# Latent attention scores: three fp32r products of high and low parts in place of one fp32 product

## The chip, the core and the metric

The kernel runs on one core of one Trainium2 chip. The metric is device time in microseconds (us) of one execution; lower is better. TensorE is called PE here, VectorE DVE, ScalarE ACT, GpSimd POOL and SyncE SP.

## The reference, cut to what matters

The whole program is two transformer mixers on 512 tokens of width 2048, all in fp32: a sliding-window attention, and then a block with two attentions side by side, a differential one and a latent one (MLA), whose outputs are gated and projected. The change touches the scores of the latent one alone: eight heads, a 128-wide part without rotation (`nope`) and a 64-wide part with rotation (`pe`), 512 tokens and 16 meta keys in front of them.

```
def _mla_attention(q_nope, q_pe, k_nope, k_pe, v):
    L = k_nope.shape[2]
    scale = (B_NOPE + B_ROPE) ** -0.5
    k_pos = jnp.arange(L, dtype=jnp.int32)

    def block(start):
        qn = lax.dynamic_slice_in_dim(q_nope, start, Q_BLOCK, axis=2)
        qp = lax.dynamic_slice_in_dim(q_pe, start, Q_BLOCK, axis=2)
        rel = (start + jnp.arange(Q_BLOCK, dtype=jnp.int32))[:, None] - k_pos[None, :]
        s = (jnp.einsum('bqhd,bkhd->bhqk', qn, k_nope) + jnp.einsum('bqhd,bkd->bhqk', qp, k_pe)).astype(jnp.float32) * scale
        s = jnp.where(rel >= 0, s, -jnp.inf)
        p = jax.nn.softmax(s, axis=-1)
        return jnp.einsum('bhqk,bkhd->bqhd', p.astype(v.dtype), v)
```

## The kernel before, in words

Every large projection is written as fp32r products of a high and a low part: ACT rounds a 128x512 weight tile to fp32r (line 1314), POOL or DVE subtracts to get the remainder (lines 1925, 2338), and PE sums hi·hi, hi·lo and lo·hi (lines 718 to 720). The attentions don't stand in the program by themselves. They are woven into projections, by step numbers written out by hand.

The latent attention runs in two rounds, i = 0 and 1, of four heads each. A round goes along with one projection of 64 steps: step Q is the three 128x512 matmuls of one of 16 weight tiles for one of 4 row blocks (`project`). Between the steps each engine's own copy of the table (`unit_time`, `turn_time`) puts in the attention's work:

- **Head turns** (`head_turn` on PE, `keep_head` on ACT). For each head, three batches of four 128x128 transposes into the PSUM bank `turn[0]`: b = 0 is q without rotation, b = 1 holds the rotated part of q, b = 2 is k without rotation. ACT copies the bank out: to `qnT` (line 1740), `qpT` (line 1743) and `knT` (line 1746). Only for b = 1 DVE makes a low part afterwards (line 2737). Head 0 has its turns after steps 6, 8 and 10, head h after steps 12h+3, 12h+6 and 12h+9.
- **Score units** (`scores_mla`). Unit u = 4·head + j, after step 12 + 3u, is the row block j of a head against (j+1)·128 + 16 keys: 144, 272, 400 or 528 columns, the last cut in 272 and 256. Each piece is `qnT`·`knT` in fp32 (line 1128, which the profile shows as two instructions), then the rotated part in fp32r against the high and the low part of its keys (lines 1129, 1130).
- DVE adds the mask and takes the maximum (`soften2`, lines 2639 and 2646), ACT takes the exponential (`weigh2`, line 1754) one step later, and three steps after the scores PE transposes the weights into `turn[0]` (`turn_p2`, lines 1164 to 1170). In units 0, 4 and 8 (`KEYS_WITH`) it also turns the 16 meta keys of the next head there (line 1168), which ACT copies to `knT` (line 1769). ACT frees the bank (`keep_pT2`). Six steps after the scores PE multiplies with the values (`values2`, lines 1191 and 1194).
- The **rotation** of head h's q is six DVE instructions (lines 2528 to 2533). It stands in DVE's queue at step 12h-3, for head 0 at step 4.

All uses of `turn[0]`, the head turns and the weights' turns, pass one after the other through the semaphore `A.free` (`s_mla_free`): `t0_use` lets PE go on only when the use before has been read out. At one step PE does, in this order: the projection, `turn_p2`, the scores, the values, the head turn. DVE does `soften2`, then `keep_o2`, `combine`, the rotation and its part of b = 1.

On POOL's queue, `attend_loads` brings the heads in from DRAM, two heads ahead. `diff_km`, the meta keys of the difference attention that follows, is loaded at step 20 of the first round (line 2073); `alibi` at step 60 of the second, after all of DVE's work on the scores (line 2076). PE transposes `diff_km` at step 2 of the difference attention (line 1202). `metaT` holds turned meta tokens for projections that are over before the latent attention begins.

Of the kernel before, what the change touches and what calls it, by code (L numbers as in the profile page):

```python
# [12 lines left out]
F32 = mybir.dt.float32  # L13
# [5 lines left out]
P = 128  # L19
# [108 lines left out]
def build(nc, a, out):  # L128
    with ExitStack() as ctx:
# [99 lines left out]
        qnT = over("qnT", [P, 2, S], B_HI + 14336)  # L229
        qpT = over("qpT", [P, 2, S], B_HI + 18432, F32R)  # L230
        knT = over("knT", [P, 2, KEYS], B_HI + 22528)
# [11 lines left out]
        metaT = sb("metaT", [P, META_UNITS, META], F32R)  # L243
# [113 lines left out]
        s_qp_hi = sem("s_qp_hi")  # L357
# [147 lines left out]
        def key_blocks(n, low):  # L505

            return km_in_q[:, n // 4, n % 4, VD + 2 * META * low:VD + 2 * META * (low + 1)]

        far_ps = turn[1][:, 3 * P:3 * P + 2 * META]

# [184 lines left out]
        def _(pe):  # L695
# [417 lines left out]
            def scores_mla(i, u):  # L1113
                head, j = u // NT, u % NT
                buf = head % 2
                if j == 0:
                    pe.wait_ge(MLA.free, i * (4 * MLA.batches + NU) + (ready_at[head] + 1))
                if j == 1 and 4 * i + head:
                    pe.wait_ge(MLA.pTm, 4 * i + head)

                pe.wait_ge(MLA.m, i * NU + u + (0 if j in (1, 2) else 1))
                q = slice(j * P, (j + 1) * P)
                start = score_at(u)
                cuts = [0, width(j)] if j < NT - 1 else [0, BANK_CUT, width(j)]
                for first, end in zip(cuts, cuts[1:]):
                    keys = slice(first, end)
                    dst = sc2[:, start + keys.start:start + keys.stop]
                    mm(dst, qnT[:, buf, q], knT[:, buf, keys], start=True, stop=False)
                    mm(dst, qpT[:, buf, q], kpeT_hi[:, keys], start=False, stop=False)
                    last = mm(dst, qpT[:, buf, q], kpeT_lo[:, keys], start=False, stop=True)  # L1130
                last.then_inc(MLA.score, 1)
# [163 lines left out]
        def _(act):  # L1295
# [430 lines left out]
            def keep_head(A, i, head, b):  # L1726
                buf = head % 2
                act.wait_ge(A.full, i * (4 * A.batches + NU) + (count["t0"] + 1))
                count["t0"] += 1
                if not A.mla:  # L1730
                    if b == 0:
                        last = nc.scalar.activation(qd_hi[:, buf], turn[0][:], ACT.Copy, scale=A_SCALE)
                    else:
                        n = 4 * i + head
                        nc.scalar.activation(kd_hi[:, buf, META:KEYS], turn[0][:], ACT.Copy)
                        last = nc.scalar.activation(kd_hi[:, buf, 0:META], km_hi[:, n * META:(n + 1) * META].bitcast(F32), ACT.Copy)
                    last.then_inc(s_d_hi, 1)
                    return
                if b == 0:
                    last = nc.scalar.activation(qnT[:, buf], turn[0][:], ACT.Copy, scale=B_SCALE)  # L1740
                elif b < A.batches - 1:

                    nc.scalar.activation(qpT[ROPE:P, buf], turn[0][ROPE:P, :], ACT.Copy, scale=B_SCALE).then_inc(s_qp_hi, 1)
                    return
                else:
                    last = nc.scalar.activation(knT[:, buf, META:KEYS], turn[0][:], ACT.Copy)
                    if head == 0:
                        last = nc.scalar.activation(knT[:, buf, 0:META], turn[1][:, 0:META], ACT.Copy)
                last.then_inc(A.free, 1)

            def weigh2(A, i, u, comp):
                lo, slot = S - (u % NT + 1) * P, u % 2 if A.mla else comp
# [4 lines left out]
            def keep_pT2(A, i, u):  # L1757
                j = u % NT
                n = (j + 1) * P
                act.wait_ge(A.full, i * (4 * A.batches + NU) + (count["t0"] + 1))  # L1760
                count["t0"] += 1
                act.wait_ge(A.pv, i * NU + (u + 1))
                if j == NT - 1:
                    nc.scalar.activation(pTm[0:META, u % 2], meta_turn(A, u), ACT.Copy).then_inc(A.pTm, 1)
                    nc.scalar.activation(pT2[:, u % 2, 0:n], turn[0][:, 0:n], ACT.Copy).then_inc(A.free, 1)
                    return
                nc.scalar.activation(pT2[:, u % 2, 0:n], turn[0][:, 0:n], ACT.Copy).then_inc(A.pT, 1)
                if A.mla and u in KEYS_WITH:
                    nc.scalar.activation(knT[:, KEYS_WITH[u] % 2, 0:META], turn[0][:, P:P + META], ACT.Copy)
                nc.scalar.activation(pTm[0:META, u % 2], meta_turn(A, u), ACT.Copy).then_inc(A.free, 1)  # L1770

            count = {"t0": 0}
# [146 lines left out]
        def _(pool):  # L1919
# [140 lines left out]
            def attend_loads(A, i, c0, then, stored=0):  # L2060

                for Q in range(4 * KC):
# [5 lines left out]
                    if A.mla and i == 0 and Q == 11:  # L2068
                        for signal in s_short:
                            pool.wait_ge(signal, 4 * 16)  # L2070
                        pool.wait_ge(s_mst, 8 * 16)
                    if A.mla and i == 0 and Q == 20:
                        pool.dma_start(diff_km[:], kv_d[S:KEYS, 0:HEADS * VD]).then_inc(s_km_in, 16)
                    if A.mla and i == 1 and Q == 60:
                        pool.wait_ge(MLA.m, 2 * NU + 1)
                        pool.dma_start(alibi[:], a["alibi"]).then_inc(s_alibi, 16)
                    if Q == 36 and stored:
                        pool.wait_ge(s_st, stored * 16)
# [40 lines left out]
        def _(dve):  # L2119
# [556 lines left out]
            def keep_o2(A, i, u):  # L2676
# [2 lines left out]
                dst = o_nat[:, bass.ds(i + (2 if A.mla else 0), 1), j, head * VD:(head + 1) * VD].rearrange("p o c -> p (o c)")  # L2679
                V.tensor_scalar(dst, turn[1][:, 2 * P:3 * P], rden_2[:, u % 4, 0:1], None, ALU.mult).then_inc(A.o, 1)  # L2680

            def low_head(i, head, b):

                buf, n = head % 2, 4 * i + head
# [26 lines left out]
            def attend_body(A, i):  # L2711
                for Q in range(4 * KC):
                    for u in range(NU):
# [3 lines left out]
                        for comp in range(A.comps):  # L2717
                            if Q == unit_time(A, u):
                                soften2(A, i, u, comp)
                    for u in range(NU):  # L2720
                        if Q == unit_time(A, u) + A.values_after:
                            keep_o2(A, i, u)
# [5 lines left out]
                    for head in range(4):  # L2728
# [4 lines left out]
                            rotate((x1, x2_), (x1, x2_), cos[:], sin[:], [rope_t[:, n] for n in range(4)]).then_inc(MLA.rope, 1)  # L2733
                            dve.wait_ge(MLA.rope, i * 4 + (head + 1))
                        if A.mla and Q == turn_time(A, head, 1):
                            dve.wait_ge(s_qp_hi, i * 4 + (head + 1))
                            V.scalar_tensor_tensor(qpT[0:ROPE, head % 2], turn[0][ROPE:P, :], B_SCALE,
                                                   qpT[ROPE:P, head % 2].bitcast(F32), ALU.mult, ALU.subtract).then_inc(MLA.free, 1)
                    for head in range(4):
                        for b in range(A.batches):  # L2740
                            if not A.mla and Q == turn_time(A, head, b):
                                low_head(i, head, b)

            for A in (MLA, DIFF):
                for i in range(2):
# [121 lines left out]
```

## Time and profile before

| | |
|---|---|
| median of 3 runs | 1600.14 us (1599.91 to 1604.0) |
| time of the profiled execution | 1600.31 us |
| its span | 1598.5 us |
| PE busy | 1578.7 us (99%) |
| PE weight loads | 1300.5 us (81%) |
| DVE, ACT, POOL busy | 885.9 (55%), 811.4 (51%), 677.0 us (42%) |
| PE's share of the chain that ended last | 92% |

A row of a timeline gives the start, the duration, the engine, the line, the operation and its tiles; in brackets stands how long the engine had been idle and what released it. Matmuls overlap, and their ends are modelled: what one costs PE is read from its start to the start of the next. PEld is the load of the stationary operand, which goes on beside the matmul ahead of it.

### The profile page before, as it was taken

How to read it: one execution, taken by the hardware profiler on the slowest of the kernel's cores; microseconds unless marked ns; L12 is line 12 of the kernel's file. 1: busy time of each engine (PE TensorE's matmuls, PEld its weight loads, DVE VectorE, ACT ScalarE, POOL GpSimd, SP SyncE). 2: the span in 40 equal slices, each digit the busy share in tenths (PEclk: the TensorE clock that was granted, in tenths of full speed). 3: DMA queues.
4: the chain of work that ended last, by engine and by line, in shares of the span. 5: the costliest groups of instructions: out<-in, count | busy, mean ns of one | idle time of the engine just before them, and what ended most of it. 6: DMA issues, size and time to landing. Idle time of an engine off the chain costs nothing.

```text
span 1598.5 us, 21759 instructions
## 1 busy us (share of the span) xinstructions
PE 1578.7 (99%) x8015; PEld 1300.5 (81%) x8015; DVE 885.9 (55%) x1837; ACT 811.4 (51%) x1686; POOL 677.0 (42%) x569
## 2 busy tenths in 40 slices
PE   9999999999999899999999999999999999999998
PEld 7788888888888688898777788888888888888886
DVE  4256767673367666458555441433345464876675
ACT  5456676663334355454435456444466665344561
POOL 5543433436676303575111024544444435664022
PEclk9999999999999999999999999999999999999999
DMA  9554755747888878958999848654655324624762
GB/s 341 148 161 93 176 130 131 181 97 168 188 191 203 184 230 267 236 175 187 253 265 279 217 139 286 206 139 134 166 143 130 110 80 136 155 80 146 248 238 105
DMA packets 139383, 285.39 MB, mean 179 GB/s; under 512 B 11228, under 2 KB 17821, under 8 KB 138605
## 3 DMA queue, kind: packets, MB, share of 16 engines
q1 hardware_dynamic: 85660, 164.49, 31.3%
q0 software_dynamic: 31664, 81.70, 25.1%
q10 hardware_dynamic: 21952, 37.81, 7.4%
q8 instruction: 64, 1.05, 0.3%
q14 instruction: 43, 0.34, 0.1%
HBM read 259.01 MB, written 92.06 MB: 220 GB/s over the span
## 4 chain that ended last, share of the span: by engine, by line
PE 92%; DVE 3%; DMA 1%; issue 1%; ACT 1%; POOL 1%; SPq 0%; POOLq 0%; DVEq 0%; ACTq 0%
PE acc L718 14%; PE acc L720 14%; PE acc L719 14%; PE acc L734 4%; PE acc L736 4%; PE acc L735 4%; PE turn L1191 3%; PE acc L888 2%; PE acc L886 2%; PE acc L887 2%; PE sc L886 2%; PE turn L886 2%; PE sc L887 2%; PE sc L888 2%; PE turn L887 2%; PE turn L888 2%
## 5 line engine op out<-in xcount | busy, mean ns | idle before, releaser
L1925 POOL TENSOR_TENSOR w_lo<-w_raw,w_hi 128x512 fp32r<-128x512 f32 x341 | 511.8, 1510 | 655.8 <-ACT w_hi L1314 654.5
L1314 ACT ACTIVATE w_hi<-w_raw 128x512 fp32r<-128x512 f32 x565 | 353.9, 629 | 450.9 <-PE acc L720 175.1
L718 PE MATMUL acc<-w_hi,setA_hi 128*128 128x512 f32 (+1 forms) x820 | 330.6, 403 | 1.0 <-POOL w_lo L1925 0.4
L720 PE MATMUL acc<-w_hi,setA_lo 128*128 128x512 f32 (+1 forms) x820 | 315.9, 385 | 0.0
L719 PE MATMUL acc<-w_lo,setA_hi 128*128 128x512 f32 (+1 forms) x820 | 314.8, 384 | 0.0
L2338 DVE TENSOR_TENSOR w_lo<-w_raw,w_hi 128x512 fp32r<-128x512 f32 x224 | 154.5, 695 | 149.0 <-ACT w_hi L1314 148.8
L720 PEld LDWEIGHTS acc<-w_hi,setA_lo 128*128 128x128 f32 x820 | 153.9, 188 | 31.7
L718 PEld LDWEIGHTS acc<-w_hi,setA_hi 128*128 128x128 f32 x820 | 154.4, 188 | 27.0 <-issue 2.9
L719 PEld LDWEIGHTS acc<-w_lo,setA_hi 128*128 128x128 f32 x820 | 154.7, 189 | 24.0
L734 PE MATMUL acc<-setA_hi,w_hi 128*128 128x512 f32 x256 | 101.9, 398 | 0.0
L736 PE MATMUL acc<-setA_lo,w_hi 128*128 128x512 f32 x256 | 99.9, 390 | 0.0
L735 PE MATMUL acc<-setA_hi,w_lo 128*128 128x512 f32 x256 | 99.7, 389 | 0.0
L718 PE MATMUL acc<-w_hi,setB_hi 128*128 128x512 f32 x192 | 77.3, 403 | 7.8 <-POOL w_lo L1925 7.7
L720 PE MATMUL acc<-w_hi,setB_lo 128*128 128x512 f32 x192 | 75.7, 394 | 0.0
L719 PE MATMUL acc<-w_lo,setB_hi 128*128 128x512 f32 x192 | 75.5, 393 | 0.0
L1417 ACT ACTIVATE p_w<-sm,negm 128x257 f32<-128x257 f32 (+1 forms) x128 | 60.5, 475 | 21.6 <-DVE negm L2193 21.4
L1754 ACT ACTIVATE p<-sm,negm 128x144 f32<-128x144 f32 (+3 forms) x96 | 54.5, 569 | 30.1 <-DVE negm L2646 18.6
L1427 ACT ACTIVATE pT<-turn 128x256 f32<-128x256 f32 (+1 forms) x64 | 34.9, 546 | 43.0 <-PE turn L838 42.9
L736 PEld LDWEIGHTS acc<-setA_lo,w_hi 128*128 128x128 f32 x256 | 48.0, 188 | 10.3
L734 PEld LDWEIGHTS acc<-setA_hi,w_hi 128*128 128x128 f32 x256 | 48.1, 188 | 9.4 <-issue 0.5
L735 PEld LDWEIGHTS acc<-setA_hi,w_lo 128*128 128x128 f32 x256 | 48.2, 188 | 9.2
L2193 DVE CUSTOM_DVE_ANT_0 sm<-sc,bias,sink_g 128x256 f32<-128x256 f32 (+1 forms) x128 | 52.1, 443 | 0.1
(551 smaller groups left out, 3244.6 us busy)
## 6 DMA issues: line engine op xcount, KB each, us to landing
w_raw<-in_swa_w_in SPq DMA_DIRECT2D x35, 1024.0 KB, 7.3
w_raw<-in_w_in SPq DMA_DIRECT2D x32, 1024.0 KB, 5.6
w_raw<-sum_out SPq DMA_DIRECT2D x64, 256.0 KB, 4.2
sum_k<-in_w_in POOLq DMA_DIRECT2D x24, 512.0 KB, 6.7
sum_out<-in_swa_w_out POOLq DMA_DIRECT2D x24, 512.0 KB, 7.6
sum_v<-in_w_in POOLq DMA_DIRECT2D x24, 512.0 KB, 8.2
w_raw<-in_w_in SPq DMA_DIRECT2D x48, 256.0 KB, 5.5
sum_out<-in_w_out POOLq DMA_DIRECT2D x24, 512.0 KB, 6.4
```

What stands on the lines that cost most here:

```text
L718: mm(acc[t][:, 0:cols], hi[:, kc, rows], wh, start=(k == 0), stop=False)
L719: mm(acc[t][:, 0:cols], hi[:, kc, rows], wl, start=False, stop=False)
L720: last = mm(acc[t][:, 0:cols], lo[:, kc, rows], wh, start=False, stop=(k == K - 1))
L734: mm(acc[t][:], wh, setA_hi[:, k], start=(k == 0), stop=False)
L735: mm(acc[t][:], wl, setA_hi[:, k], start=False, stop=False)
L736: last = mm(acc[t][:], wh, setA_lo[:, k], start=False, stop=(k == KC - 1))
L886: mm(dst, hi, wh, start=start, stop=False)
L887: mm(dst, hi, wl, start=False, stop=False)
L888: last = mm(dst, lo, wh, start=False, stop=stop)
L1314: nc.scalar.activation(w_at(f)[0], raw_of(f), ACT.Copy).then_inc(done, 1)
L1925: nc.gpsimd.tensor_tensor(lo, raw_of(f), hi.bitcast(F32), ALU.subtract).then_inc(s_lo, 1)
L2338: V.tensor_tensor(lo, raw_of(f), hi.bitcast(F32), ALU.subtract).then_inc(s_wlo, 1)
```

## The change

`qnT` and `knT` become fp32r tiles `qn_hi` and `kn_hi`, which ACT writes as before. DVE gets two new functions, `low_nope` and `low_meta_keys`, that subtract the high part from what stands in PSUM and write `qn_lo` and `kn_lo`. The fp32 product becomes three fp32r products. `A.free` of these uses now comes from DVE, after ACT has signalled `s_mla_hi`. The low parts lie over `metaT`, where also `diff_km` lies, so the load of `diff_km` goes from step 20 of the first round to step 60 of the second, ahead of `alibi`.

```
+        metaT, META_T = place("metaT", [P, META_UNITS, META], F32R)
+        qn_lo = over("qn_lo", [P, 2, S], META_T, F32R)
+        kn_lo = [over("kn_lo0", [P, KEYS], META_T + 4096, F32R), over("kn_lo1", [P, KEYS], B_HI + 26752, F32R)]
...
-                    mm(dst, qnT[:, buf, q], knT[:, buf, keys], start=True, stop=False)
+                    mm(dst, qn_hi[:, buf, q], kn_hi[:, buf, keys], start=True, stop=False)
+                    mm(dst, qn_hi[:, buf, q], kn_lo[buf][:, keys], start=False, stop=False)
+                    mm(dst, qn_lo[:, buf, q], kn_hi[:, buf, keys], start=False, stop=False)
                     mm(dst, qpT[:, buf, q], kpeT_hi[:, keys], start=False, stop=False)
...
                 if b == 0:
-                    last = nc.scalar.activation(qnT[:, buf], turn[0][:], ACT.Copy, scale=B_SCALE)
+                    last = nc.scalar.activation(qn_hi[:, buf], turn[0][:], ACT.Copy, scale=B_SCALE)
...
-                last.then_inc(A.free, 1)
+                last.then_inc(s_mla_hi, 1)
...
                 if A.mla and u in KEYS_WITH:
-                    nc.scalar.activation(knT[:, KEYS_WITH[u] % 2, 0:META], turn[0][:, P:P + META], ACT.Copy)
+                    nc.scalar.activation(kn_hi[:, KEYS_WITH[u] % 2, 0:META], turn[0][:, P:P + META], ACT.Copy)
+                    nc.scalar.activation(pTm[0:META, u % 2], meta_turn(A, u), ACT.Copy).then_inc(s_mla_hi, 1)
+                    return
...
-                    if A.mla and i == 0 and Q == 20:
-                        pool.dma_start(diff_km[:], kv_d[S:KEYS, 0:HEADS * VD]).then_inc(s_km_in, 16)
                     if A.mla and i == 1 and Q == 60:
                         pool.wait_ge(MLA.m, 2 * NU + 1)
+                        pool.dma_start(diff_km[:], kv_d[S:KEYS, 0:HEADS * VD]).then_inc(s_km_in, 16)
                         pool.dma_start(alibi[:], a["alibi"]).then_inc(s_alibi, 16)
...
+            def low_nope(i, head, b):
+
+                buf = head % 2
+                dve.wait_ge(s_mla_hi, mla_hi_count(i, (head, b)))
+                if b == 0:
+                    last = V.scalar_tensor_tensor(qn_lo[:, buf], turn[0][:], B_SCALE, qn_hi[:, buf].bitcast(F32),
+                                                  ALU.mult, ALU.subtract)
+                else:
+                    if head == 0:
+                        V.tensor_tensor(kn_lo[buf][:, 0:META], turn[1][:, 0:META], kn_hi[:, buf, 0:META].bitcast(F32), ALU.subtract)
+                    last = V.tensor_tensor(kn_lo[buf][:, META:KEYS], turn[0][:], kn_hi[:, buf, META:KEYS].bitcast(F32), ALU.subtract)
+                last.then_inc(MLA.free, 1)
+
+            def low_meta_keys(i, u):
+
+                buf = KEYS_WITH[u] % 2
+                dve.wait_ge(s_mla_hi, mla_hi_count(i, u))
+                V.tensor_tensor(kn_lo[buf][:, 0:META], turn[0][:, P:P + META], kn_hi[:, buf, 0:META].bitcast(F32),
+                                ALU.subtract).then_inc(MLA.free, 1)
```

In the tables, `low_meta_keys` stands after `soften2` of the same step and `low_nope` at the end of its step. Lines in the rows of the changed kernel are its own.

DVE's queue at the opening of the first round, steps 8 to 12 (`rope_t` is the rotation, `sm` and `negm` the masked scores and their maximum); before:

```order
L2737 SCALAR_TENSOR_TENSOR qpT<-turn,qpT 64x512 [waits s_qp_hi,s_mla_rope]
L2528 TENSOR_TENSOR rope_t<-nat_q,cos 128x128 [waits s_mla_ld_qk1]
L2529 TENSOR_TENSOR rope_t<-nat_q,sin 128x128
L2530 TENSOR_TENSOR rope_t<-nat_q,sin 128x128
L2531 TENSOR_TENSOR rope_t<-nat_q,cos 128x128
L2532 TENSOR_TENSOR nat_q<-rope_t 128x4x32 [waits s_d]
L2533 TENSOR_TENSOR nat_q<-rope_t 128x4x32
L2639 MEMSET tick 128x1 [waits s_mla_score,s_mst,s_mla_rope]
L2646 ISA sm_103,negm_168<-sc,mask 128x144
L2646 ISA negm_168 128x1
L2669 RECIPROCAL rden_171<-den_170 128x1 [waits s_mla_p]
```

and in the changed kernel, from step 6 on:

```order
L2700 SCALAR_TENSOR_TENSOR qn_lo<-turn,qn_hi 128x512 [waits s_mla_hi,s_mla_rope]
L2773 SCALAR_TENSOR_TENSOR qpT<-turn,qpT 64x512 [waits s_mla_hi]
L2541 TENSOR_TENSOR rope_t<-nat_q,cos 128x128 [waits s_mla_ld_qk1]
L2542 TENSOR_TENSOR rope_t<-nat_q,sin 128x128
L2543 TENSOR_TENSOR rope_t<-nat_q,sin 128x128
L2544 TENSOR_TENSOR rope_t<-nat_q,cos 128x128
L2545 TENSOR_TENSOR nat_q<-rope_t 128x4x32 [waits s_d]
L2546 TENSOR_TENSOR nat_q<-rope_t 128x4x32
L2704 TENSOR_TENSOR kn_lo_139<-turn,kn_hi 128x16 [waits s_mla_hi,s_mla_rope]
L2705 TENSOR_TENSOR kn_lo_139<-turn,kn_hi 128x512
L2652 MEMSET tick 128x1 [waits s_mla_score,s_mst]
L2659 ISA sm_103,negm_171<-sc,mask 128x144
```

A subtraction for q came ahead of b = 1, and two for k came behind the rotation of head 1 and ahead of the first `soften2`.

DVE's queue from step 15 of the first round on; before:

```order
L2639 MEMSET tick 128x1 [waits s_mla_score,s_d]
L2646 ISA sm_103,negm_168<-sc,mask 128x272
L2646 ISA negm_168 128x1
L2669 RECIPROCAL rden_171<-den_170 128x1 [waits s_mla_o,s_mla_p]
L2639 MEMSET tick 128x1 [waits s_mla_score,s_d]
```

and in the changed kernel:

```order
L2652 MEMSET tick 128x1 [waits s_mla_score,s_d]
L2659 ISA sm_103,negm_171<-sc,mask 128x272
L2659 ISA negm_171 128x1
L2712 TENSOR_TENSOR kn_lo_140<-turn,kn_hi 128x16 [waits s_mla_hi]
L2700 SCALAR_TENSOR_TENSOR qn_lo<-turn,qn_hi 128x512 [waits s_mla_hi]
L2682 RECIPROCAL rden_174<-den_173 128x1 [waits s_mla_o,s_mla_p]
L2652 MEMSET tick 128x1 [waits s_mla_score,s_d]
```

The subtraction of the meta keys came behind the second unit's `soften2` (272 columns), and that of head 1's q behind it.

POOL's queue at the end of the second round (`nat_v` and `natm_v` are values of the difference attention); before:

```order
L2044 DMA natm_v<-kv_d 16x128
L1925 TENSOR_TENSOR w_lo<-w_raw,w_hi 128x512 [waits s_hi] x3
L2076 DMA alibi<-in_alibi 128x1344 [waits s_mla_m]
L2043 DMA nat_v<-kv_d 128x4x128 [waits s_mla_pv]
L2044 DMA natm_v<-kv_d 16x128
```

and in the changed kernel:

```order
L2058 DMA natm_v<-kv_d 16x128
L1939 TENSOR_TENSOR w_lo<-w_raw,w_hi 128x512 [waits s_hi] x3
L2088 DMA diff_km<-kv_d 16x1024 [waits s_mla_m]
L2089 DMA alibi<-in_alibi 128x1344
L2057 DMA nat_v<-kv_d 128x4x128 [waits s_mla_pv]
```

The load of `diff_km` came in ahead of that of `alibi`, and took over its wait.

## Rows read from the trace of the kernel before

**Rows 1.** Window of both rounds: length, busy PE, PEld, DVE, ACT, POOL, PEclk, DMA, GB/s.

```profile
1003.00:1172.00 169.00, 168.55 (x989) 141.85 (x988) 54.69 (x220) 78.15 (x203) 79.03 (x89) 1.00 0.54 156
```

**Rows 2.** Timeline of TensorE: score units of 144, 272 + 256 and 400 columns, and what follows.

```profile
1011.51 0.41 PE L1128 MATMUL sc<-knT,qnT 128*128 128x144 f32 x2
1011.82 0.27 PE L1130 MATMUL sc<-kpeT_lo,qpT 128*128 128x144 f32 x1
1011.93 0.44 PE L718 MATMUL acc<-w_hi,setA_hi 128*128 128x512 f32 x1
...
1107.26 0.62 PE L1128 MATMUL sc<-knT,qnT 128*128 128x272 f32 x2
1107.84 0.28 PE L1130 MATMUL sc<-kpeT_lo,qpT 128*128 128x272 f32 x1
1107.97 0.59 PE L1128 MATMUL sc<-knT,qnT 128*128 128x256 f32 x2
1108.52 0.28 PE L1130 MATMUL sc<-kpeT_lo,qpT 128*128 128x256 f32 x1
1108.64 0.60 PE L1191 MATMUL turn<-nat_v,pT 128*128 128x128 f32 x4
...
1120.98 0.84 PE L1128 MATMUL sc<-knT,qnT 128*128 128x400 f32 x2
1121.84 0.34 PE L1130 MATMUL sc<-kpeT_lo,qpT 128*128 128x400 f32 x1
1122.02 0.38 PE L1191 MATMUL turn<-nat_v,pT 128*128 128x128 f32 x2
```

**Rows 3.** The DVE subtraction with one PSUM operand, by line: minimum, median and maximum ns.

```profile
L2691 DVE TENSOR_TENSOR kd_lo<-turn,kd_hi x8: 680/684/687, 1176.4 to 1303.1; 128x512 fp32r<-128x512 f32 x8
```

**Rows 4.** Timeline, opening of the second round (DVE, ACT and TensorE).

```profile
1090.61 0.60 ACT L1740 ACTIVATE qnT<-turn 128x512 f32<-128x512 f32 x1 [1.85 <-PE turn L1100]
1091.74 0.60 PE L1103 MATMUL turn<-ident,nat_q 128*128 128x128 f32 x4
...
1093.07 0.69 DVE L2737 SCALAR_TENSOR_TENSOR qpT<-turn,qpT 64x512 fp32r<-64x512 f32 x1 [4.18 <-ACT qpT L1743]
1093.82 0.66 PE L1094 MATMUL turn<-ident,nat_k 128*128 128x128 f32 x4
1095.17 0.18 ACT L1748 ACTIVATE knT<-turn 128x16 f32<-128x16 f32 x1
1096.06 0.41 PE L1128 MATMUL sc<-knT,qnT 128*128 128x144 f32 x2
```

**Rows 5.** Timeline, opening of the first round (DVE, POOL and TensorE).

```profile
1007.36 3.77 POOL L1925 TENSOR_TENSOR w_lo<-w_raw,w_hi 128x512 fp32r<-128x512 f32 x3
1009.23 2.06 DVE L2528 TENSOR_TENSOR rope_t<-nat_q,cos 128x128 f32<-128x128 f32 x1
1013.17 0.28 DVE L2533 TENSOR_TENSOR nat_q<-rope_t 128x128 f32<-128x128 f32 x1
1014.50 0.28 PE L1164 MATMUL turn<-ident,p 128*16 128x128 f32 x1 [0.27 <-ACT p L1754]
```

**Rows 6.** Timeline, step 15 of the second round.

```profile
1099.96 0.63 PE L1100 MATMUL turn<-ident,nat_q 128*128 128x128 f32 x4
1100.55 0.08 DVE L2646 DVE_READ_ACCUMULATOR2_ANT negm<- 128x1 f32 x1
```

**Rows 7.** Timeline, steps 21 to 24 of the second round.

```profile
1111.03 0.28 DVE L2533 TENSOR_TENSOR nat_q<-rope_t 128x128 f32<-128x128 f32 x1
1111.82 0.27 PE L1164 MATMUL sc<-ident,p 128*16 128x128 f32 x1
```

**Rows 8.** Timeline and DMA landings: start of the difference attention; below, landings of line 2033.

```profile
1166.05 0.59 POOL L2076 DMA_DIRECT2D alibi<-in_alibi  x1
1171.86 0.66 PE L1202 MATMUL turn<-ident,diff_km 16*128 16x16 f32 x8
...
DMA to landing us min/median/max: 3.2/4.5/9.5
```

More of the change, by code:

```diff
@@ L228, in build @@
         nat_v = over("nat_v", [P, 2, NT, VD], B_HI + 10240)
-        qnT = over("qnT", [P, 2, S], B_HI + 14336)
+        qn_hi = over("qn_hi", [P, 2, S], B_HI + 14336, F32R)
         qpT = over("qpT", [P, 2, S], B_HI + 18432, F32R)
-        knT = over("knT", [P, 2, KEYS], B_HI + 22528)
+        kn_hi = over("kn_hi", [P, 2, KEYS], B_HI + 22528, F32R)
         qd_hi = over("qd_hi", [P, 2, S], B_HI + 14336, F32R)
@@ L242, in build @@
         rope_t = over("rope_t", [P, 4, NT, ROPE // 2], WORK + 5120)
-        metaT = sb("metaT", [P, META_UNITS, META], F32R)
+        metaT, META_T = place("metaT", [P, META_UNITS, META], F32R)
+        qn_lo = over("qn_lo", [P, 2, S], META_T, F32R)
+        kn_lo = [over("kn_lo0", [P, KEYS], META_T + 4096, F32R), over("kn_lo1", [P, KEYS], B_HI + 26752, F32R)]
         alibi_h = over("alibi_h", [P, 2, ALIBI_AT[NT]], MASK)
@@ L356, in build @@
         s_lam, s_alibi, s_fin_w, s_x1in, s_h2, s_fin = (sem("s_" + n) for n in ("lam", "alibi", "fin_w", "x1in", "h2", "fin"))
-        s_qp_hi = sem("s_qp_hi")
+        s_mla_hi = sem("s_mla_hi")
         s_km_in, s_km_ps, s_km = sem("s_km_in"), sem("s_km_ps"), sem("s_km")
@@ L507, in key_blocks, with mla_hi_count @@
             return km_in_q[:, n // 4, n % 4, VD + 2 * META * low:VD + 2 * META * (low + 1)]
+        mla_his = sorted([(turn_time(MLA, h, b), 1, (h, b)) for h in range(4) for b in range(MLA.batches)]
+                         + [(unit_time(MLA, u) + MLA.turn_after, 0, u) for u in KEYS_WITH], key=lambda e: e[:2])
+        mla_hi_at = {what: n + 1 for n, (_, _, what) in enumerate(mla_his)}
+        def mla_hi_count(i, what):
+            return i * len(mla_his) + mla_hi_at[what]
         far_ps = turn[1][:, 3 * P:3 * P + 2 * META]
@@ L1739, in keep_head @@
                 if b == 0:
-                    last = nc.scalar.activation(qnT[:, buf], turn[0][:], ACT.Copy, scale=B_SCALE)
+                    last = nc.scalar.activation(qn_hi[:, buf], turn[0][:], ACT.Copy, scale=B_SCALE)
                 elif b < A.batches - 1:
-                    nc.scalar.activation(qpT[ROPE:P, buf], turn[0][ROPE:P, :], ACT.Copy, scale=B_SCALE).then_inc(s_qp_hi, 1)
+                    nc.scalar.activation(qpT[ROPE:P, buf], turn[0][ROPE:P, :], ACT.Copy, scale=B_SCALE).then_inc(s_mla_hi, 1)
                     return
                 else:
-                    last = nc.scalar.activation(knT[:, buf, META:KEYS], turn[0][:], ACT.Copy)
+                    last = nc.scalar.activation(kn_hi[:, buf, META:KEYS], turn[0][:], ACT.Copy)
                     if head == 0:
-                        last = nc.scalar.activation(knT[:, buf, 0:META], turn[1][:, 0:META], ACT.Copy)
-                last.then_inc(A.free, 1)
+                        last = nc.scalar.activation(kn_hi[:, buf, 0:META], turn[1][:, 0:META], ACT.Copy)
+                last.then_inc(s_mla_hi, 1)
             def weigh2(A, i, u, comp):
@@ L2719, in attend_body @@
                                 soften2(A, i, u, comp)
+                    for u in KEYS_WITH if A.mla else ():
+                        if Q == unit_time(A, u) + A.turn_after:
+                            low_meta_keys(i, u)
                     for u in range(NU):
@@ L2735, in attend_body @@
                         if A.mla and Q == turn_time(A, head, 1):
-                            dve.wait_ge(s_qp_hi, i * 4 + (head + 1))
+                            dve.wait_ge(s_mla_hi, mla_hi_count(i, (head, 1)))
                             V.scalar_tensor_tensor(qpT[0:ROPE, head % 2], turn[0][ROPE:P, :], B_SCALE,
@@ L2742, in attend_body @@
                                 low_head(i, head, b)
+                            elif A.mla and b != 1 and Q == turn_time(A, head, b):
+                                low_nope(i, head, b)
             for A in (MLA, DIFF):
```

## The prediction

> **What bounds the kernel now.** I read the window of the two rounds first, since nothing outside of it is edited but one load. PE is busy in 168.55 of 169.00 us at the full granted clock (1.00, the 2.4 GHz level), while DVE has 54.69, ACT 78.15 and POOL 79.03 us of work [rows 1]. So PE is the path here: what its instructions get shorter is gained one for one, and what PE waits longer is lost one for one. The other engines have room in their sums; what counts is when they hand `turn[0]` back. After that I read the timelines: PE's own score units, then at each use of `turn[0]` that follows a head turn how much later than now PE would get the bank.
>
> **The three products.** What a matmul costs is the step from its start to the next start. A unit of 144 columns now takes 1011.93 - 1011.51 = 0.42 us, one of 272 takes 1107.97 - 1107.26 = 0.71, one of 400 takes 1122.02 - 1120.98 = 1.04, and one of 528 takes 1108.64 - 1107.26 = 1.38: 3.55 us for a head [rows 2]. One fp32r matmul behind another is line 1130: 0.11 us at 144 columns, 0.12 at 256, 0.13 at 272, 0.18 at 400 [rows 2]. With five of them a piece, 144 columns take 0.55 us (slower than now: the step does not shrink with the columns any more), 272 take 0.65, 400 take 0.90, 528 take 1.25: 3.35 us. That is 0.20 us a head. The rows are rounded to 0.01 and enter five times, so the ends are 0.1 and 0.35 us; I take 0.22, and for 8 heads **-1.8 us** (ends -0.8 and -2.8). Taken apart, the fp32 product of 272 columns costs about 0.71 - 2 x 0.13 = 0.45 us, against 0.39 for three fp32r ones [rows 2].
> The Trainium skill (FP8 and Floating Point Precision, TensorE Precision Notes) gives true fp32 as four passes through the array. Three passes for four, over 8 x 1344 columns at one a cycle of 2.4 GHz, would save an estimated 4.5 us, and the sum below would be 2.7 us lower by it. The row at 272 columns bears out the direction and half of the size (0.06 us against 0.11), the row at 144 columns speaks against it; I go by the rows.
>
> **The new DVE work.** The nearest operation is line 2691, the same subtraction with one operand in PSUM: 0.68 us, between 0.680 and 0.687 eight times [rows 3]; the scaled form takes 0.69 [rows 4]. For the 16 meta columns no DVE row of that form is shown; it lies between 0.08 us (an accumulator read of one column, [rows 6]) and 0.18 us (ACT's copy of as many columns, [rows 4]), and I take 0.15. In all 16 large and 8 small ones, 12.2 us: DVE's 54.69 us have room for that, so its work as such costs nothing. ACT writes fp32r in place of fp32 and does no more than before: nothing. What costs is that DVE now gives the bank back, in its own order. A handover from DVE to PE takes 0.06 us (1093.07 + 0.69 to 1093.82, where PE waited, [rows 4]); from ACT to DVE I take 0.1.
>
> - **Before b = 1 of head 0 (step 8), both rounds.** ACT ends at 1091.21; with 0.1 + 0.69 + 0.06 PE gets the bank at 1092.06 and not at 1091.74 [rows 4]: +0.32, twice, **+0.6**. The wait for b = 1 behind it stands as before.
> - **Before the first unit (step 12), second round.** ACT ends at 1095.35, now 0.32 later; with 0.1 + 0.15 + 0.68 + 0.06 PE starts at 1096.66. It would have come at 1096.06 + 0.32 = 1096.38 [rows 4]: **+0.3**.
> - **The same, first round.** Here the subtraction stands behind the rotation of head 1, which ends only at 1013.17 + 0.28 = 1013.45, long after PE's first unit at 1011.51 [rows 2, 5]. Nobody on PE waits for that now. Then 0.15 + 0.68 + 0.06, so PE starts at about 1014.35, 2.84 us late, 0.32 of which is counted. Behind it PE waits 0.27 us less at 1014.50, as the exponential is then ahead [rows 5]. So +2.25, if the rotation ends where it does now. The low end is the +0.3 of the second round. **+2.2**.
> - **Step 15, both rounds.** PE turned head 1's q at 1099.96, right behind the scores. Now the bank comes back only when DVE has gone through `soften2` of the second unit, to 1100.63, and has subtracted the meta keys: 1100.63 + 0.15 + 0.06 = 1100.84 [rows 6]. +0.88, twice, **+1.8**. For heads 2 and 3 (steps 27 and 39) ten value instructions of 128 columns stand between scores and turn; at 0.11 us each (the step at 144 columns, [rows 2]) their 1.1 us cover the chain of 0.88, so 0 (high end 0.1 each).
> - **Steps 24 and 36, four times.** The subtraction for k stands behind the next head's rotation, which ends at 1111.31: plus 0.68 + 0.06 is 1112.05, against 1111.82 [rows 7]: +0.23, **+0.9**. For head 3 no rotation comes ahead, and ACT, DVE and two handovers (0.6 + 0.1 + 0.68 + 0.06) fit within the three steps of nine matmuls that PE has: 0. The same covers b = 0 of heads 1 to 3.
> - **`diff_km`.** POOL issues it at 1166.05, and PE wants it at 1171.86, 5.8 us later [rows 8]. Loads of 16 rows on this queue land in 3.2 to 9.5 us, 4.5 in the median [rows 8]: 0 at the median, 3.7 us at the worst. `alibi` is issued about half a microsecond later; ACT reads it, with nothing due on PE behind it for over a microsecond: 0.
>
> Sum: -1.8 + 0.6 + 0.3 + 2.2 + 1.8 + 0.9 = +4.0 us. On the profiled execution, 1600.31 us (span 1598.5), that gives 1604.3; the median lies 0.17 us below that execution, so **1604.1 us**, 0.25% above 1600.14. About 0.3%, or 4.8 us, is what a measurement of this kernel can tell from no change; the forecast is just within.
>
> **Rivals.**
> 1. *The first round's rotation gets through earlier.* DVE's first rotation instruction took 2.06 us against 0.28 for the last of its kind, and ended when POOL's run of three (1007.36 + 3.77 = 1011.13) was over; the other five took until 1013.45, so one of them was held as well [rows 5]. The first hold stays. The second is a meeting with one more POOL subtraction of 1.3 us (a third of 3.77), which hangs on ACT and so on PE, and moves 0.32 us later with it. If the rest of the rotation now slips in ahead, PE starts the first unit some 1.2 us earlier: 1602.9. The Trainium skill (SBUF — State Buffer, Who interferes with whom) states that a DVE instruction with two SBUF inputs and a GpSimd instruction that reads SBUF hold the port for a whole instruction, whichever was first. By that rule, the row on the first instruction agrees, and a shift of 0.32 us is enough to turn the second meeting. Chance 0.25, within 0.3%.
> 2. *The stalls add up to more, or `diff_km` comes late* (the other side). The mechanism: `diff_km` lands after 5.8 us, since it is now issued beside weight loads and the store of a projection's output; PE stands at line 1202, in order, with everything behind it. It decides from a landing of 5.8 us, and costs up to 3.7: at a landing of 7.5 us +1.7, 1605.8. Or without it: the first opening at 2.6 and the meta subtraction at its upper end give +0.9 in all, 1605.0. For it speaks that my sum is 0.8 us below the bound already; against it the median landing. Chance 0.36, slower.
> 3. *Full gain of the passes, small stalls* (faster). If the pass count held (-4.5) and the first opening cost only its low end of 0.3, the sum would be -4.5 + 0.6 + 0.3 + 0.3 + 1.8 + 0.9 = -0.6: 1599.5, still no change. For over 0.3% faster the stalls would have to be gone as well, and PE's queue is in order. Chance 0.04.
>
> **How the numbers follow.** The forecast itself has 0.35, rival 1 has 0.25, rival 2 0.36, rival 3 0.04. Within 0.3% is the forecast and rival 1: 0.60. Slower is rival 2: 0.36. Faster: 0.04. The range goes from 1599.8 (the larger gain of 2.8 us with the first opening at its low end of 0.3 gives 1601.2, rival 3 gives 1599.5; the low end is near the latter) to 1607.5 (the sum with a `diff_km` 3.4 us late).
>
> **What would show it.** In the changed profile: units of about 0.55, 0.65, 0.90 and 1.25 us from start to start; no fp32 matmul among the scores; a PE wait of over 2 us, released by the DVE subtraction for k, before the first unit of the first round; 0.9 us before head 1's q in both rounds, released by the meta subtraction; 0.2 us four times behind a rotation. It would be wrong if PE idles at line 1202's successor, if the first opening shows no long wait, or if five fp32r matmuls of 144 columns take less than the 0.42 us of now.

## The result, and the profile after

| | before | changed |
|---|---|---|
| median of 20 runs | 1600.88 us (1599.84 to 1604.0) | 1604.82 us (1601.76 to 1608.97) |
| ratio | | 1.0023 (95% interval 1.0016 to 1.0030) |
| the profiled execution | 1600.31 us, span 1598.5 us | 1605.59 us, span 1603.8 us |

The kernel became slower by 0.16 to 0.30%: within 0.3%, but not nothing. Forecast were 1604.1 us and "within 0.3%".

The page of the changed kernel shows hardly anything: PE still fills the span, DVE has 11.2 us more, and the mean granted clock is 0.996 against 0.997.

```profile
span 1603.8 us, 21868 instructions
...
PE 1580.4 (99%) x8055; PEld 1303.9 (81%) x8055; DVE 897.1 (56%) x1861; ACT 811.6 (51%) x1686; POOL 678.6 (42%) x569
```

The window of the two rounds shows more (changed kernel, columns as in [rows 1]; its ends are the same times as before, though the changed kernel runs some us later). PE was busy in 168.55 of 169.00 us before; now 4.59 us are idle, and DVE's work went from 54.69 to 65.24 us:

```profile
1003.00:1172.00 169.00, 164.41 (x1007) 140.21 (x1006) 65.24 (x244) 75.90 (x200) 77.78 (x88) 1.00 0.52 149
```

What ended PE's idle times stands in the view of the waits, from 1000 to 1185 us (engine, tile and line, releaser: us in total, times, longest). The rows of PE are time that the matmuls stood still; those of PEld are idle time of the weight loads, which partly lies under a matmul and is not added to it. All five below are new. The only wait of PE's matmuls of over 0.1 us that this stage had before, 0.27 us for the exponential [rows 5], is gone.

```profile
PEld sc L1138 <- DVE kn_lo L2705: 2.2, 2, 1.7
PE turn L1110 <- DVE kn_lo L2712: 1.7, 2, 0.9
PE sc L1138 <- DVE kn_lo L2705: 1.3, 1, 1.3
PE sc L1176 <- DVE kn_lo L2705: 1.2, 4, 0.5
PEld turn L1113 <- DVE qn_lo L2700: 1.2, 2, 0.6
```

To compare kernels more finely than medians allow, I measure **the stage**: from the last product of the meta tokens (line 748 before, 758 after), which the attention does not touch yet, to the turn of `diff_km`. For the kernel before, it takes two rows of TensorE's timeline, the one below and the second of [rows 8]: 1171.86 - 999.58 = 172.28 us.

```profile
999.58 0.40 PE L748 MATMUL sc<-w_lo,ckvmT 128*96 128x512 f32 x1
```

In the changed kernel it takes 175.55 us, **+3.27**. Two kernels that are the same in the stage agree there to 0.01 us (`eC_km` below: 172.29), although the part ahead of it differs from one execution to the next: it ended at 999.58 before and 1.77 us later in the changed kernel, with no edit ahead of it. So the 5.3 us between the spans of the two profiled executions are 3.3 us in the stage, 1.8 us ahead of it and 0.2 us behind it.

The 1.8 us ahead of it have two main sources, neither of them edited: 1.5 us more were gone by the matmul that stood at 17.55 us before, and another 0.6 us came between 544 and 547 us, where the stretch at the lower level of the granted clock lasted longer (mean granted clock from 525 to 550 us: 0.86 before, 0.80 in the changed kernel). The slow start stands in four of the six kept executions with DVE's subtractions and in none of the four without, the longer stretch in four of the six and in two of the four. The medians speak for chance: over the six kernels with the subtractions (all runs are below) their differences to before exceed those of the stage by 0.3 us on average, and 0.2 of that have their place behind the stage.

The 0.2 us behind the stage do come with the change. PE waits at 1327.66 us for a DVE instruction that began 0.29 us late, with no releaser that the profile shows ("issue"):

```profile
1327.22 0.17 DVE L2669 CUSTOM_DVE_ANT_0 sm<-turn,alibi_h 128x16 f32<-128x16 f32 x1 [0.29 <-issue]
1327.66 0.46 PE L1203 MATMUL turn<-nat_v,pT 128*128 128x128 f32 x2 [0.20 <-DVE negm_far L2669]
```

From `diff_km` to the last matmul the six kernels with DVE's subtractions take 0.19 to 0.27 us more than before, the three others -0.01 to +0.09. In all, the change costs about 3.5 us; the medians differ by 3.9 us (interval 2.6 to 4.8), which goes with that.

### The profile page after: what moved, and what is told of

Its sections match the earlier page's. It is cut to its first block, busy times and chain, and to the rows that moved or that the text cites. A ratio compares the mean times of both kernels' runs of the same rounds, so it can differ in the third digit from the quotient of the medians.

```text
span 1603.8 us, 21868 instructions
## 1 busy us (share of the span) xinstructions
PE 1580.4 (99%) x8055; PEld 1303.9 (81%) x8055; DVE 897.1 (56%) x1861; ACT 811.6 (51%) x1686; POOL 678.6 (42%) x569
## 4 chain that ended last, share of the span: by engine, by line
PE 91%; DVE 3%; DMA 1%; issue 1%; ACT 1%; POOL 1%; SPq 0%; POOLq 0%; DVEq 0%; ACTq 0%
PE acc L728 14%; PE acc L730 14%; PE acc L729 13%; PE acc L744 4%; PE acc L746 4%; PE acc L745 4%; PE turn L1203 2%; PE acc L898 2%; PE acc L896 2%; PE acc L897 2%; PE sc L896 2%; PE turn L896 2%; PE sc L897 2%; PE turn L897 2%; PE sc L898 2%; PE turn L898 2%
```

## The experiments

Two theories were at issue. **Mine**: the three products gain about 2 us, and handing `turn[0]` back by DVE costs more, by DVE's order of work. **The rival**: the loads and the order of DMA (`diff_km`), or a larger gain and a larger loss than I had. The ratio of each run is that of its median to the median of before on the same chip, with the 95% interval; "stage" is the measure above, and its difference is taken from the one kept trace of before.

### The products alone

All that DVE does for the low parts is taken out, ACT frees the bank as before, and all three products use the high parts; the low parts are left out of the result.

```
-                    mm(dst, qn_hi[:, buf, q], kn_lo[buf][:, keys], start=False, stop=False)
-                    mm(dst, qn_lo[:, buf, q], kn_hi[:, buf, keys], start=False, stop=False)
+                    mm(dst, qn_hi[:, buf, q], kn_hi[:, buf, keys], start=False, stop=False)
+                    mm(dst, qn_hi[:, buf, q], kn_hi[:, buf, keys], start=False, stop=False)
...
-                last.then_inc(s_mla_hi, 1)
+                last.then_inc(A.free, 1)
```

> The changed kernel without the low parts: no subtraction on DVE for q and k without rotation, the bank is freed by ACT as before, and the three fp32r products all take the high parts (the scores are those of three times the high product). It has the new matmuls and none of the new waits. Theory 1 (the products gain, the later return of the bank loses): the four unit sizes together get 0.30 us a head shorter, 8 heads 2.4 us, so about 1598.4 us beside a before of 1600.9, ratio 0.9985, and no PE wait of over 0.3 us in the two rounds. Rival A (five short fp32r matmuls are no faster than the fp32 pair, the loss is theirs): 1601 to 1604 us, ratio 1.000 or above.

Measured: 0.9982 (0.9973 to 0.9991), stage 170.16, -2.12 us. All of it lies in the units. First comes TensorE's timeline of the changed kernel in the second round, whose units have the sizes of this run to 0.02 us where no wait follows them. A unit is best read from the start of the transpositions ahead of it to the start of the instruction behind it: from turn to first product the rows show 0.35 us here and 0.44 before, so the first fp32r product seems to be recorded 0.09 us early.

```profile
1111.99 0.49 PE L1182 MATMUL turn<-ident,p 128*128 128x128 f32 x3
1112.23 0.37 PE L1138 MATMUL sc<-kn_hi,qn_hi 128*128 128x272 f32 x1
...
1113.40 0.28 PE L1142 MATMUL sc<-kpeT_lo,qpT 128*128 128x256 f32 x1
1113.52 0.60 PE L1203 MATMUL turn<-nat_v,pT 128*128 128x128 f32 x4
...
1117.19 0.60 PE L1182 MATMUL turn<-ident,p 128*128 128x128 f32 x4
1117.54 0.32 PE L1138 MATMUL sc<-kn_hi,qn_hi 128*128 128x144 f32 x1
1117.69 0.27 PE L1139 MATMUL sc<-kn_lo,qn_hi 128*128 128x144 f32 x1
1117.80 0.28 PE L1140 MATMUL sc<-kn_hi,qn_lo 128*128 128x144 f32 x1
...
1118.03 0.28 PE L1142 MATMUL sc<-kpeT_lo,qpT 128*128 128x144 f32 x1
1118.14 0.88 PE L1203 MATMUL turn<-nat_v,pT 128*128 128x128 f32 x6
```

and before, for 528 and 144 columns:

```profile
1106.93 0.49 PE L1170 MATMUL turn<-ident,p 128*128 128x128 f32 x3
...
1111.93 0.60 PE L1170 MATMUL turn<-ident,p 128*128 128x128 f32 x4
1112.37 0.41 PE L1128 MATMUL sc<-knT,qnT 128*128 128x144 f32 x2
...
1112.80 0.43 PE L1191 MATMUL turn<-nat_v,pT 128*128 128x128 f32 x2
```

From the turn on, 144 columns cost 1112.80 - 1111.93 = 0.87 us before and 1118.14 - 1117.19 = 0.95 now; 528 cost 1108.64 - 1106.93 = 1.71 [rows 2] and now 1113.52 - 1111.99 = 1.53. In the run with the products alone the median unit differs from before by +0.09 us at 144 columns, -0.09 at 272 (0 for head 0's, where a head turn follows at the same distance), -0.13 at 400 and -0.16 at 528. With 8 units of each size, of which 6 at 272 count: 0.72 - 0.53 - 1.04 - 1.28 = -2.1 us, the whole stage difference. The theory that the gain is that of the pass count, 4.5 us, falls.

### DVE's work and waits alone

Everything of the change stays but the three products: they are one fp32 product of the high parts (the low parts are computed and not used).

```
-                    mm(dst, qn_hi[:, buf, q], kn_hi[:, buf, keys], start=True, stop=False)
-                    mm(dst, qn_hi[:, buf, q], kn_lo[buf][:, keys], start=False, stop=False)
-                    mm(dst, qn_lo[:, buf, q], kn_hi[:, buf, keys], start=False, stop=False)
+                    mm(dst, qn_hi[:, buf, q].bitcast(F32), kn_hi[:, buf, keys].bitcast(F32), start=True, stop=False)
```

> The changed kernel with its DVE subtractions, its semaphores and its loads, but with one fp32 product of the high parts in place of three fp32r ones (the low parts of q and k are computed and not used). It has the new waits and the old matmuls. Theory 1: the waits cost their 5.4 to 5.9 us and nothing is gained, so about 1606.6 us, ratio 1.0035. Rival A: the loss goes away with the products, so 1601 to 1602 us, ratio below 1.001.

Measured: 1.0029 (1.0018 to 1.0041), stage 177.91, +5.63 us. Its waits are those of the changed kernel, to 0.1 us:

```profile
PE turn L1110 <- DVE kn_lo L2710: 1.7, 2, 0.9
PE sc L1138 <- DVE kn_lo L2703: 1.3, 1, 1.3
PE sc L1174 <- DVE kn_lo L2703: 1.2, 4, 0.5
```

The two halves add up: -2.1 + 5.6 = +3.5, against +3.3 together, which is 0.2 us less. What the change gains and what it costs are two things that nearly add up.

### The load of `diff_km` alone

The kernel before, with this load issued at step 60 of the second round.

```
-                    if A.mla and i == 0 and Q == 20:
-                        pool.dma_start(diff_km[:], kv_d[S:KEYS, 0:HEADS * VD]).then_inc(s_km_in, 16)
...
+                        pool.dma_start(diff_km[:], kv_d[S:KEYS, 0:HEADS * VD]).then_inc(s_km_in, 16)
                         pool.dma_start(alibi[:], a["alibi"]).then_inc(s_alibi, 16)
```

> The kernel before, with the load of diff_km alone moved to step 60 of the second round, ahead of that of alibi. Theory 1: it lands before PE wants it, no change, ratio 0.9995 to 1.0005. Rival B (the late load and the later alibi cost): a PE wait at the transposes of diff_km, or ACT late behind alibi, and a ratio of 1.001 or more (over 1.6 us).

Measured: 1.0002 (0.9993 to 1.0010), stage 172.29, +0.01 us. Nothing, and the rival with the late load falls. In the changed kernel POOL issued it at 1171.08, PE turned it without a wait at 1176.90, 5.8 us later. ACT waited 0.37 us for `alibi`; no wait of PE follows from that:

```profile
1171.08 0.54 POOL L2088 DMA_DIRECT2D diff_km<-kv_d  x1
1175.51 0.42 ACT L1798 ACTIVATE alibi_h<-alibi,slopes 128x144 f32<-128x144 f32 x1 [0.37 <-DMA alibi<-in_alibi]
1176.90 0.66 PE L1214 MATMUL turn<-ident,diff_km 16*128 16x16 f32 x8
```

### DVE's order, both places

If the costs are DVE's order, they must go when the order is changed and nothing else. The rotation of heads 1 to 3 goes behind the subtraction for k, and the meta keys' subtraction ahead of `soften2` of its step.

```
-                        if A.mla and Q == max(12 * head - 3, 4):
+                        if A.mla and Q == (4, 13, 23, 35)[head]:
...
             def attend_body(A, i):
                 for Q in range(4 * KC):
+                    for u in KEYS_WITH if A.mla else ():
+                        if Q == unit_time(A, u) + A.turn_after:
+                            low_meta_keys(i, u)
...
-                    for u in KEYS_WITH if A.mla else ():
-                        if Q == unit_time(A, u) + A.turn_after:
-                            low_meta_keys(i, u)
```

> The changed kernel with DVE's queue in another order and nothing else changed: the rotation of heads 1, 2 and 3 stands at steps 13, 23 and 35 (was 9, 21 and 33), behind the subtraction for k, and the subtraction of the meta keys stands ahead of the mask and maximum of its step (was behind). Theory 1 (the place in DVE's queue makes the waits): the waits before the first unit of the first round (1.4), at step 24 and 36 (4 x 0.38) go, that at step 15 shrinks from 0.9 to about 0.3 twice, 4 us in all, so about 1600.8 us, ratio 1.000. Rival C (the waits come from the length of the subtractions, 0.68 us more on each return, wherever they stand): 1603.5 to 1605 us, ratio 1.002.

Measured: 0.9997 (0.9988 to 1.0006), stage 171.25, -1.03 us; 4.3 us below the changed kernel. Its waits in the stage:

```profile
PE turn L1110 <- DVE kn_lo L2712: 0.7, 2, 0.3
PE turn L1113 <- DVE qn_lo L2700: 0.2, 1, 0.2
PEld sc L1138 <- DVE kn_lo L2705: 0.8, 2, 0.4
```

The wait before the first unit fell from 1.3 us to none, those at steps 24 and 36 are gone, that at step 15 fell from 0.86 to 0.33 us. By medians this kernel can't be told from before: its interval holds 1.

### The rotation's place alone

Of the two edits above only the first.

> The changed kernel with one half of the reordering: the rotation of heads 1, 2 and 3 stands at steps 13, 23 and 35 (was 9, 21 and 33), the meta subtraction stays behind the mask and maximum. Theory 1: the waits at the first unit of the first round and at steps 24 and 36 go (1.2 + 1.5 us), those at step 15 stay (0.9 twice). From the first head turn to the turn of diff_km it takes 166.9 to 167.3 us (169.83 in the changed kernel, 166.57 before, 165.53 with both halves), ratio to before 1.0003 to 1.0008. Rival D (the one half does all of it): 165.5 us and ratio 0.9997.

Measured: 1.0003 (0.9994 to 1.0012), stage 172.29, +0.01 us, which is 3.26 below the changed kernel and lower than I had expected: the two openings give back 1.4 us of it (the first round's 1.3), and steps 24 and 36 give back 1.8, where I had counted 1.5 (see below). The meta keys' place is worth the other 1.04: twice the 0.53 us by which the idle time before head 1's q differs between the two runs. Here is `eD_rot`, then `eF_both`:

```profile
1019.89 0.63 PE L1110 MATMUL turn<-ident,nat_q 128*128 128x128 f32 x4 [0.86 <-DVE kn_lo L2712]
```

```profile
1017.02 0.63 PE L1110 MATMUL turn<-ident,nat_q 128*128 128x128 f32 x4 [0.33 <-DVE kn_lo L2712]
```

### ACT alone frees the bank of the meta keys

On top of `eF_both`, the 16 meta keys are turned into an unused end of the scores' bank, so that `turn[0]` is free when ACT has copied the weights, without waiting for DVE's subtraction. ACT copies the weights' part first, and ahead of the units with j = 2 PE waits for one more of DVE's maxima (`MLA.m`).

```
-                    nc.tensor.transpose(turn[0][:, P:P + META], natm_k[:, head % 2], ident[0:META, 0:META])
+                    nc.tensor.transpose(sc[0][:, CW - META:CW], natm_k[:, head % 2], ident[0:META, 0:META])
...
-                pe.wait_ge(MLA.m, i * NU + u + (0 if j in (1, 2) else 1))
+                pe.wait_ge(MLA.m, i * NU + u + (0 if j == 1 else 1))
```

> On top of both halves of the reordering: the 16 meta keys of heads 1 to 3 are turned into the free end of the other score bank instead of turn[0], so that ACT alone gives turn[0] back there and the meta subtraction is on nobody's way. Theory 1: the two waits of 0.35 us at step 15 go, so 164.8 us from the first head turn to the turn of diff_km (165.53 without it), ratio to before about 0.9993. If these waits were something else than the return of the bank, nothing changes: 165.5.

Measured: 0.9994 (0.9985 to 1.0002), stage 170.59, 0.66 us shorter again, which is the two waits of 0.33; in its trace the row of line 1110 no longer has one.

### Head 0's turns earlier, with the change and without

On top of `eG_act`, head 0's three batches stand after steps 4, 7 and 10 in place of 6, 8 and 10; only b = 1 waits for the rotation. PE, ACT and DVE then have three steps for a use of the bank and not two.

```
-                return 6 + 2 * b if A.mla else 2 + 3 * b
+                return 4 + 3 * b if A.mla else 2 + 3 * b
```

> On top of that: head 0 has its turns at steps 4, 7 and 10 (was 6, 8 and 10), and b = 0 waits for the load of q and not for the rotation, which only b = 1 reads. Three steps of nine matmuls (2.06 us) then stand between two uses of the bank, as everywhere else, and the chain from turn to return takes 2.07 to 2.2 us. Theory 1: the new waits before b = 1 (0.33 twice) go, and the old ones before b = 2 (0.5 twice, there before the change as well) and before the first b = 0 (0.3) with them: 1.5 to 1.9 us less than without it, ratio to before 0.998 to 0.9985. If the chain is longer than three steps: 0.5 us or less.

Measured: 0.9983 (0.9974 to 0.9992), 1599.27 us against 1601.99, stage 169.34, -2.94 us, of which 1.25 are this last step. This version beats both kernels. In the window PE has no idle time left:

```profile
1003.00:1172.00 169.00, 169.00 (x1046) 146.01 (x1046) 68.72 (x246) 80.15 (x206) 81.04 (x91) 1.00 0.56 159
```

Is that the change, or would the kernel before gain the same from earlier turns? The same edit on the kernel before:

> The kernel before with the earlier turns of head 0 alone, no fp32r products: what of the last step has nothing to do with the change. Theory 1: the old waits go, 2 x 0.5 + 0.3 us, so 165.3 us from the first step to the turn of diff_km where it was 166.6, ratio 0.9990 to 0.9995. If those waits cost nothing because PE catches up later: ratio 1.000.

Measured: 0.9998 (0.9989 to 1.0006), stage 172.11, -0.17 us. I had expected over a microsecond: a miss. The waits ahead of b = 0 and b = 2 did go, but I had read them from the weight loads, 0.3 and twice 0.5 us. PE gained only 0.33 us up to the first unit of the first round and 0.24 in the second round, and in the first round it then only came earlier to a wait that stayed. The timeline, opening of the first round:

```profile
1009.30 2.73 DVE L2530 TENSOR_TENSOR rope_t<-nat_q,cos 128x128 f32<-128x128 f32 x1
...
1012.36 1.38 DVE L2533 TENSOR_TENSOR rope_t<-nat_q,cos 128x128 f32<-128x128 f32 x1
...
1014.75 0.41 ACT L1756 ACTIVATE p<-sm,negm 128x144 f32<-128x144 f32 x1 [2.73 <-DVE negm L2648]
1015.31 0.28 PE L1166 MATMUL turn<-ident,p 128*16 128x128 f32 x1 [0.71 <-ACT p L1756]
```

The rotation of head 1 still stands ahead of the first `soften2`, so the exponential comes no earlier, and PE's wait for it grew from 0.27 [rows 5] to 0.71 us, which took back all of the 0.33 us. With the rotation moved (`eH_turns`) that wait is not there. So in the first round the earlier turns pay only together with DVE's new order. Of the 2.94 us, 2.1 are the products; the kernel before with both of DVE's and PE's moves was not run, so how much of the remaining 0.8 it would have had as well stays open.

## Why the prediction was right, and where it was not

The forecast of 1604.1 us, 4.0 above before, stands against a stage difference of 3.3 and medians 3.9 apart. The sign of each term was right; four sizes were not, and one wait of 0.3 us was not in the sum at all.

- **The products** (-1.8): -2.1 by `eA_products`. The step from start to start, and that it does not shrink below 0.11 us at 144 columns, was the right thing to read; 144 columns did become slower, by 0.09 us. Five rows rounded to 0.01 us were only good to 0.3 us. The unit lengths that I gave as a sign (0.55, 0.65, 0.90 and 1.25) are 0.60, 0.71, 0.99 and 1.29 from start to start, in part because the first product is recorded early; the differences read from the neighbours are what holds. The Trainium skill's four passes for fp32 (FP8 and Floating Point Precision, TensorE Precision Notes) would have given an estimated 4.5 us; the runs show less than half of that.
- **Step 8** (+0.6): from head 0's b = 0 to b = 1 PE needs 1009.28 - 1007.07 = 2.21 us in the first round, against 1.87 before, and 2.14 against 1.83 in the second. +0.65, right. Before:

```profile
1005.29 0.66 PE L1100 MATMUL turn<-ident,nat_q 128*128 128x128 f32 x4
...
1007.16 0.38 PE L1103 MATMUL turn<-ident,nat_q 128*128 128x128 f32 x2
```

- **The first unit, second round** (+0.3): +0.2 by the recorded start of the unit, +0.3 by the start of the matmul behind it, less the 0.09 of the products. Right.
- **The first unit, first round** (+2.2): this step of the sum failed, and rival 1 took place. The changed kernel:

```profile
1007.07 0.66 PE L1110 MATMUL turn<-ident,nat_q 128*128 128x128 f32 x4
...
1009.13 3.77 POOL L1939 TENSOR_TENSOR w_lo<-w_raw,w_hi 128x512 fp32r<-128x512 f32 x3
1009.28 0.66 PE L1113 MATMUL turn<-ident,nat_q 128*128 128x128 f32 x4 [0.16 <-DVE qn_lo L2700]
1011.32 1.74 DVE L2541 TENSOR_TENSOR rope_t<-nat_q,cos 128x128 f32<-128x128 f32 x1
...
1013.70 0.29 DVE L2545 TENSOR_TENSOR nat_q<-rope_t 128x128 f32<-128x128 f32 x1
1013.90 1.42 POOL L1939 TENSOR_TENSOR w_lo<-w_raw,w_hi 128x512 fp32r<-128x512 f32 x1 [1.00 <-ACT w_hi L1326]
1013.91 0.28 DVE L2546 TENSOR_TENSOR nat_q<-rope_t 128x128 f32<-128x128 f32 x1
...
1014.32 0.68 DVE L2705 TENSOR_TENSOR kn_lo<-turn,kn_hi 128x512 fp32r<-128x512 f32 x1
1015.06 0.33 PE L1138 MATMUL sc<-kn_hi,qn_hi 128*128 128x144 f32 x1 [1.29 <-DVE kn_lo L2705]
```

and the kernel before at the same place:

```profile
1011.81 1.29 POOL L1925 TENSOR_TENSOR w_lo<-w_raw,w_hi 128x512 fp32r<-128x512 f32 x1 [0.68 <-ACT w_hi L1314]
1011.92 1.32 DVE L2532 TENSOR_TENSOR nat_q<-rope_t 128x128 f32<-128x128 f32 x1
```

Before, POOL's subtraction began 0.11 us ahead of the fifth rotation instruction, which then took 1.32 us. Now it begins 0.20 us behind it, and the same instruction takes 0.29. A shift of 0.31 us, about the 0.32 by which b = 1 comes later, turned the meeting, and the fifth instruction took 1.03 us less. PE waits 1.29 us and not over 2. From the first head turn to the first unit it takes 1015.06 - 1007.07 = 7.99 us against 1011.51 - 1005.29 = 6.22; less 0.34 counted in step 8 and 0.27 that the exponential no longer costs, the term is +1.16, where rival 1 had about 1.0. The Trainium skill (SBUF — State Buffer, Who interferes with whom) says that such a pair blocks for a whole instruction, whichever was first; the four rows agree (DVE 1.32 us behind POOL, and 0.29 ahead of it, with POOL then at 1.42 us in place of 1.29). I gave it 0.25 and it should have been the forecast: a meeting decided by 0.11 us does not stand a shift of 0.32, and both numbers were to be had from the trace of before.
- **Step 15** (+1.8): PE idles 0.86 us before line 1110 twice, released by the meta keys' subtraction. Right as a wait; that subtraction took 0.17 us, where I took 0.15. Beside `eA_products`, where the unit ahead of head 1's q gained nothing either, the two waits cost PE 0.8 us each, 1.6 in all.
- **Steps 24 and 36** (+0.9): some +0.37 three times and +0.70 at step 36 of the second round, 1.8 in all, twice the forecast. Step 24 of the second round:

```profile
1115.92 0.28 DVE L2546 TENSOR_TENSOR nat_q<-rope_t 128x128 f32<-128x128 f32 x1
...
1116.24 0.69 DVE L2705 TENSOR_TENSOR kn_lo<-turn,kn_hi 128x512 fp32r<-128x512 f32 x1
...
1117.08 0.27 PE L1176 MATMUL sc<-ident,p 128*16 128x128 f32 x1 [0.20 <-DVE kn_lo L2705]
```

From the last score product PE needs 1117.08 - 1113.40 = 3.68 us, against 1111.82 - 1108.52 = 3.30 before [rows 2, 7]. The chain is the one that I had, but the handover is 1117.08 - 1116.93 = 0.15 us and not 0.06, and the subtraction begins 0.04 us after the rotation's end. The idle time shown (0.20) is less than the loss, because the modelled end of a matmul covers part of it. At step 36 of the second round the chain began later: DVE stood still for 0.33 us between two instructions of the same `soften2`, with no releaser in the profile, and the rotation, the subtraction and PE behind it came as much later.

```profile
1132.04 0.06 DVE L2652 MEMSET tick<- 128x1 f32 x1 [2.29 <-PE sc L1142]
1132.43 0.71 DVE L2659 CUSTOM_DVE_ANT_0 sm<-sc,mask 128x528 f32<-128x528 f32 x1 [0.33 <-issue]
1135.62 0.27 PE L1176 MATMUL sc<-ident,p 128*16 128x128 f32 x1 [0.54 <-DVE kn_lo L2705]
```

`eB_dve` has the same pause and the same wait of 0.54 us; before has 0.08 us from the one instruction to the other, and `eD_rot` and `eF_both`, with the rotation elsewhere, have no such pause at this place. Like the 0.29 us behind the stage, such a pause stands only in kernels with DVE's subtractions. No run shows what makes it. The prediction had no term for it.
- **`diff_km`** (0): 0, by `eC_km`.

Together -2.1 + 0.65 + 0.3 + 1.16 + 1.6 + 1.8 = +3.4, against 3.27 measured; the rest is in differences of under 0.07 us each between the changed kernel and `eA_products`. The predicted sum of 4.0 was 0.7 too high: 1.0 for the meeting, 0.3 for the products and 0.2 at step 15, less 0.9 at steps 24 and 36. So the agreement of the sum (4.0) with the medians (3.9) is partly luck: errors of opposite sign nearly cancelled, the cost behind the stage was not foreseen, and the interval goes from 2.6 to 4.8. The 0.7 us between 1604.1 and the measured median of 1604.82 are those by which the 20 runs of before lie above the 1600.14 from which I counted.

## What to carry to other kernels

Moving a buffer's release to another engine costs by that engine's queue order more than by its work: DVE had room for 11 us of new work, and the 5.6 us that the move cost came through what stood ahead of a few instructions (4.3 us, by `eF_both`) and through the length of the subtractions where PE waits for the bank at once, as at step 8 (0.3 us each time). Ask of each new release what is ahead of it in that queue, and move that, before counting the gain of the change that wanted it; here putting the rotation and one subtraction elsewhere was worth 4.3 us, and turned a slower kernel into one that is 0.17% faster than before with two further moves. A wait that is removed on its own may only bring the engine earlier to the next one.

## What was not expected

- The handover from DVE to PE has two sizes that repeat to 0.01 us: 0.06 before lines 1113 and 1138, 0.15 before lines 1110 and 1176. At 1110 and 1176 the instruction also waits for a second condition (the rotation, the exponential), which had long been met; but line 1138 has a second one too. What makes the difference was not tried.
- Here a delay of 0.3 us upstream shortened DVE's chain by one microsecond, as it turned the order of a DVE and a POOL instruction.
- Pauses of DVE of 0.3 us with no releaser came with the change, at two places, and each cost PE time: 0.3 us at step 36 and 0.2 us behind the stage. None of the four kernels without the subtractions has one in these parts, so the added instructions are suspected; that was not tested.
- Two executions of kernels that are alike in a stage take the same time there to 0.01 us, while the 1000 us ahead of it differed by up to 3 us between executions, in part by the length of a stretch at the lower clock. A stage that is measured between two instructions of one engine tells effects apart that medians of 11 runs (intervals of 0.09% to each side, 1.4 us) cannot.
